# Up projection of a decoder layer: one run of high and low x, and high- and low-weight matmuls by turns

## The reference

```python
    n = rmsnorm(h, mlp_norm_w[l])
    h = h + jnp.square(jax.nn.relu(n @ w_up[l])) @ w_down[l]
return rmsnorm(h, final_norm_w)
```

## Time and profile before

| | |
|---|---|
| median of the timed runs | 1051.15 us |
| profiled execution, span from first to last instruction | 1050.2 us |
| what lies around the span (median less span) | 0.95 us |
| PE busy | 1037.8 us, 99% |
| weight loads (PEld), beside PE | 896.9 us, 85% |
| DVE busy | 637.0 us, 61% |
| ACT busy | 503.3 us, 48% |
| DMA | 190.42 MB, mean 181 GB/s |
| matmuls of L1805 and L1808 | 1024 each |

### The profile page before, as it was taken

The page is one execution under the profiler, slowest core; times in us unless marked ns, Lnnn a source line. Parts: engine busy times, 40 slices in busy tenths (PEclk is TensorE's granted clock), DMA queues, the critical chain, the costliest instruction groups (busy, mean ns, idle before and its releaser), DMA issues.

```text
span 1050.2 us, 14384 instructions
## 1 busy us (share of the span) xinstructions
PE 1037.8 (99%) x5631; PEld 896.9 (85%) x5631; DVE 637.0 (61%) x762; ACT 503.3 (48%) x630; POOL 92.5 (9%) x152
## 2 busy tenths in 40 slices
PE   8999999999999999999999999999999999999996
PEld 7889999888888888888888888888888888888885
DVE  4655986988856554565456456545554555655666
ACT  4655855877754544344334333334433433433434
POOL 2135100633200100000000000000000000000002
PEclk9999999999999999999999999999999999999999
DMA  9576672342346566566556655665566556655662
GB/s 329 181 201 196 210 251 82 133 147 91 111 127 192 164 187 191 186 198 195 186 182 197 197 178 187 197 197 180 184 198 194 182 186 196 197 175 189 199 200 80
DMA packets 89137, 190.42 MB, mean 181 GB/s; under 512 B 8758, under 2 KB 29964, under 8 KB 88716
## 3 DMA queue, kind: packets, MB, share of 16 engines
q1 hardware_dynamic: 88668, 189.41, 56.7%
q10 hardware_dynamic: 432, 0.52, 0.1%
HBM read 187.82 MB, written 2.10 MB: 181 GB/s over the span
## 4 chain that ended last, share of the span: by engine, by line
PE 94%; DVE 3%; ACT 2%; issue 1%; DMA 0%; DVEq 0%; ACTq 0%
PE ps L1805 23%; PE ps L1387 15%; PE ps L1388 15%; PE ps L1391 15%; PE ps L1808 12%; PE ps L1678 2%; PE ps L1679 1%; PE ps L1682 1%; PE ps L1662 1%; PE ps L1460 1%; PE ps L1635 1%; PE ps L1663 1%; PE ps L1513 1%; PE ps L1511 1%; PE ps L1512 1%
## 5 line engine op out<-in xcount | busy, mean ns | idle before, releaser
L885 DVE TENSOR_TENSOR w_lo<-raw,w_hi 128x2048 fp32r<-128x2048 f32 (+4 forms) x198 | 402.3, 2034 | 355.0 <-ACT w_hi L594 289.1
L594 ACT ACTIVATE w_hi<-raw 128x2048 fp32r<-128x2048 f32 x119 | 228.1, 1917 | 399.3 <-PE ps L1391 200.7
L1805 PE MATMUL ps<-xT,w_hi 128*128 128x512 f32 x1024 | 279.3, 394 | 0.0
L1805 PEld LDWEIGHTS ps<-xT,w_hi 128*128 128x128 f32 x1024 | 176.0, 189 | 24.3
L1808 PEld LDWEIGHTS ps<-xT,w_lo 128*128 128x128 f32 x1024 | 157.1, 189 | 21.7
L1387 PE MATMUL ps<-w_hi,hidT 128*128 128x512 f32 x448 | 174.5, 390 | 0.0
L1388 PE MATMUL ps<-w_lo,hidT 128*128 128x512 f32 x448 | 174.4, 389 | 0.0
L1808 PE MATMUL ps<-xT,w_lo 128*128 128x256 f32 x1024 | 162.8, 281 | 0.0
L1391 PE MATMUL ps<-w_hi,hidT 128*128 128x512 f32 x448 | 138.1, 389 | 0.0
L587 ACT ACTIVATE w_hi<-raw 128x1024 fp32r<-128x1024 f32 (+3 forms) x75 | 104.1, 1391 | 68.0 <-PE ps L1391 40.9
L1391 PEld LDWEIGHTS ps<-w_hi,hidT 128*128 128x128 f32 x448 | 84.1, 188 | 17.6
(11 more groups left out here) (339 smaller groups left out, 1268.8 us busy)
## 6 DMA issues: line engine op xcount, KB each, us to landing
raw<-in_w_up SPq DMA_DIRECT2D x64, 1024.0 KB, 5.2
raw<-in_w_down SPq DMA_DIRECT2D x64, 1024.0 KB, 5.4
raw<-in_w_o SPq DMA_DIRECT2D x16, 1024.0 KB, 5.5
raw<-in_w_in SPq DMA_DIRECT2D x8, 1024.0 KB, 5.3
raw<-in_w_in SPq DMA_DIRECT2D x8, 816.0 KB, 4.4
raw<-in_w_in SPq DMA_DIRECT2D x6, 832.0 KB, 8.8
raw<-in_mla_w_uq SPq DMA_DIRECT2D x12, 256.0 KB, 4.6
raw<-in_mla_w_ukv SPq DMA_DIRECT2D x4, 512.0 KB, 4.8
```

Of the source, the lines that this page charges most:

```text
L594: act.activation(w_hi[:, j % SPLIT, :], raw[:, j % RAW, :], ACT.Copy).then_inc(hi_done, 1)
L885: return dve.tensor_tensor(dst, src, high.bitcast(F32), ALU.subtract)
L1805: pe.matmul(both, w_hi[:, slot, 512 * b + P * f:512 * b + P * f + P], xT[:, :, k0 + b, :], start=start and b == 0, stop=False)
```

## The change

`xT` is declared with the part inside the block, so that the low part of a block lies directly behind its high part; all writers and readers have their indices turned. In `up_products` the moving operand of L1805 is then one run of 512 elements and not two of 256, and the destination is the whole bank in one run; the two loops over `b` become one, in which the high-weight matmul and the low-weight matmul of a block follow each other.

```diff
-        xT, Y_AT = seq(X_AT, ("xT", [P, 2, KT, T], F32R))
+        xT, Y_AT = seq(X_AT, ("xT", [P, KT, 2, T], F32R))
...
-                act.activation(xT[:, 0, k, :], bank(4 + k % 4, T), ACT.Copy, scale=wcols[:, k:k + 1]).then_inc(xt_hi, 1)
+                act.activation(xT[:, k, 0, :], bank(4 + k % 4, T), ACT.Copy, scale=wcols[:, k:k + 1]).then_inc(xt_hi, 1)
...
-                return xT[:, part, k, P * t:P * t + P]
+                return xT[:, k, part, P * t:P * t + P]
...
-                        pe.matmul(o, w_hi[:, s, w], xT[:, 0, k, :], start=k == 0 and f == 0, stop=False)
-                        m = pe.matmul(o, w_hi[:, s, w], xT[:, 1, k, :], start=False, stop=False)
+                        pe.matmul(o, w_hi[:, s, w], xT[:, k, 0, :], start=k == 0 and f == 0, stop=False)
+                        m = pe.matmul(o, w_hi[:, s, w], xT[:, k, 1, :], start=False, stop=False)
...
                 for f in range(4):
                     if free is not None:
                         free(f)
-                    both = ps[:, b0 + f, :].rearrange("p (c t) -> p c t", c=2)
                     for b in range(4):
-                        pe.matmul(both, w_hi[:, slot, 512 * b + P * f:512 * b + P * f + P], xT[:, :, k0 + b, :],
+                        w = slice(512 * b + P * f, 512 * b + P * f + P)
+                        pe.matmul(ps[:, b0 + f, :], w_hi[:, slot, w], xT[:, k0 + b, :, :].rearrange("p c t -> p (c t)"),
                                   start=start and b == 0, stop=False)
-                    for b in range(4):
-                        m = pe.matmul(ps[:, b0 + f, 0:T], w_lo[:, slot, 512 * b + P * f:512 * b + P * f + P], xT[:, 0, k0 + b, :],
+                        m = pe.matmul(ps[:, b0 + f, 0:T], w_lo[:, slot, w], xT[:, k0 + b, 0, :],
                                       start=False, stop=stop and b == 3)
                 m.then_inc(w_used, 1)
```

More of the change, by code:

```diff
@@ L774, in turned_hi @@
                 act.wait_ge(ht_t, k + 1)
-                act.activation(xT[:, 0, k, :], bank(4 + k % 4, T), ACT.Copy,
+                act.activation(xT[:, k, 0, :], bank(4 + k % 4, T), ACT.Copy,
                                scale=wcols[:, PRM["mlp"] + k:PRM["mlp"] + k + 1]).then_inc(ht_hi, 1)
@@ L908, in x_lo @@
                 dve.wait_ge(xt_hi, k + 1)
-                low(xT[:, 1, k, :], bank(4 + k % 4, T), xT[:, 0, k, :], wcols[:, k:k + 1]).then_inc(xt_lo, 1)
+                low(xT[:, k, 1, :], bank(4 + k % 4, T), xT[:, k, 0, :], wcols[:, k:k + 1]).then_inc(xt_lo, 1)
             def c_lo(k):
@@ L1207, in turned_lo @@
                 dve.wait_ge(ht_hi, k + 1)
-                low(xT[:, 1, k, :], bank(4 + k % 4, T), xT[:, 0, k, :], wcols[:, PRM["mlp"] + k:PRM["mlp"] + k + 1]).then_inc(ht_lo, 1)
+                low(xT[:, k, 1, :], bank(4 + k % 4, T), xT[:, k, 0, :], wcols[:, PRM["mlp"] + k:PRM["mlp"] + k + 1]).then_inc(ht_lo, 1)
             for c in range(WO_N + 4, MLP0):
@@ L1677, in q_products @@
                         w = slice(256 * b + P * f, 256 * b + P * f + P)
-                        pe.matmul(o, w_hi[:, s, w], xT[:, 0, k, :], start=k == 0 and f == 0, stop=False)
-                        m = pe.matmul(o, w_hi[:, s, w], xT[:, 1, k, :], start=False, stop=False)
+                        pe.matmul(o, w_hi[:, s, w], xT[:, k, 0, :], start=k == 0 and f == 0, stop=False)
+                        m = pe.matmul(o, w_hi[:, s, w], xT[:, k, 1, :], start=False, stop=False)
                         if c == WO_M - 1 and quarter == 3 and k == KT - 1:
                             m.then_inc(first_done, 1)
-                        m = pe.matmul(o, w_lo[:, s, w], xT[:, 0, k, :], start=False, stop=k == KT - 1 and f == 1)
+                        m = pe.matmul(o, w_lo[:, s, w], xT[:, k, 0, :], start=False, stop=k == KT - 1 and f == 1)
                     if quarter == 1 and c in FREED:
```

## The result

The changed kernel takes 1053.06 us (median of 18 runs, 1052.34 to 1054.38) against 1051.29 for the kernel before (18 runs, 1050.93 to 1052.62): ratio 1.0017, 95% interval 1.0010 to 1.0023. It is slower by 1.8 us; the forecast was 2.8 us, 1053.9 us in all, with a range of 1052.3 to 1055.5. The profiled execution has a span of 1050.9 us against 1050.2.

The account below looks back on a forecast made before the run. PE, busy 99% of the 1050.2 us span, was taken as the bound. Order +2.8, layout 0 and elsewhere 0 gave 1053.0; 0.95 around the span made 1053.9 us, own range 1052.3 to 1055.5, wider range 1046.6 to 1056.0.

Parts of the forecast that it names:

- PE bounds, so only start to start counts: Whole kernel: PE busy 99% of the span, never waiting in the loop, so only intervals between matmul starts set the price.
- Its signs: Loop timeline: sixteen pairs in 5.65 us, first 512 behind a down projection still 227 ns; a shorter loop refutes the prediction.
- Layout at zero: Up projection's moving operand as one run instead of two 16 KB apart: no gain, bounded above by 6 us.
- The second rival: Up projection: cost hangs on shares of widths, not order; 350.7 ns a pair stays, 1051.2 us; chance 0.22.
- Its estimate that a load of 107 ns is hidden: Up projection: a 128-column weight load takes 107 ns, as long as a 256 streams, so hidden in either order.
- a worse alternation: Up projection: each 512 at 237 ns, each 256 at 120, 355 ns a pair or more; +6.4 us, 1057.6; chance 0.08.
- Order: toll of 6.7 ns a pair: Up projection: alternation costs 6.7 ns over unmixed prices, as in the input projection; 353.4 against 350.7 ns a pair, +2.8 us.
- On 1024 pairs: Up projection: the extra 2.7 ns was applied to all 1024 pairs of high- and low-weight matmuls, giving +2.8 us.
- No wait changes: Whole kernel: no wait, transfer or semaphore changes and the weight slot's release stays on the last low-weight matmul; 0 us.
- The first rival: Up projection: single 256s between 512s never build up the excess; 346.7 ns a pair, 4.1 us faster, 1047.0; chance 0.28.
- "The finer the two are mixed, the dearer": Rule from the input projection's 512s and 320s: strict alternation costs 6.7 ns a pair, a coarser order 3 ns.

Follow-up runs that it names:

- PE alone: Small kernel without the layer, TensorE only: sections of matmul orders, mostly behind 24 matmuls of 512 columns; alternation took 352.8 ns a pair, or 346.6 behind one transpose.
- sixteen and sixteen: Changed kernel's layout, but each chunk runs all sixteen 512-column matmuls, then all sixteen 256-column ones; 1048.85 us, ratio 0.9977 to the kernel before.
- the snake: Like sixteen and sixteen, but odd chunks begin with their 256-column matmuls, so chunks meet in equal width; 1047.96 us, ratio 0.9967 to the kernel before.
- two and two: Changed kernel's layout, each output tile ordered as two 512s, two 256s, two 512s, two 256s; 1048.90 us, ratio 0.9976 to the kernel before.
- four and four: Order of the kernel before: four 512-column matmuls, then four 256-column ones, per output tile; 350.7 ns a pair, 1051.29 us.
- one transpose: Changed kernel plus one 128-column transpose ahead of each of the loop's 14 up projections; 1051.33 us, ratio 0.9999 to the kernel before.

## Why the prediction was right, and where its size was off

- *PE bounds, so only start to start counts.* Right: PE isn't idle in the loop in any kernel here, and each time followed from the sum of its intervals. Its signs came as written: sixteen pairs in 5.65 us (22.60/4), the first 512 behind a down projection at 0.23 us, and the loop longer and not shorter.
- *Layout at zero.* Right, and shown twice: 1.0000 with the layout alone, equal totals on PE alone.
- *The second rival (order doesn't matter, 350.7 ns a pair either way)* fell: the order alone took the loop to 353.3 and the kernel to 1.0015 (1.0006 to 1.0024). Its estimate that a load of 107 ns is hidden beside any 256 doesn't fit the runs: a load's record lasts 0.19 us, and the price of a pair depends on how wide the loads are (353.1 with 128 columns, 340.0 with 64). The fourth, *a worse alternation* from 355 ns up, wasn't reached.
- *Order: toll of 6.7 ns a pair, taken from the 512/320 alternation.* 353.4 forecast, 353.3 measured in all thirteen up projections behind the first down projection. Borrowing the toll across widths came out by luck as much as by reason: 288 beside 512 has half of it and 224 half as much again, while 320 and 384 have the same.
- *On 1024 pairs.* This factor was mis-sized: it holds for 13 x 64 + 16 = 848. Of the 192 pairs ahead of the first down projection only the first chunk's 16 pay it, since the others entered from transposes (eight each time, and eight gave the cheap cycle on PE alone too). So 848 pairs pay 2.6 ns more than before and 176 pay 4 ns less: 2.2-0.7 = +1.5 us, where 2.8 was forecast and 1.8 was measured. So the slowdown stayed at 0.17%, under the 0.2% that the prediction held for somewhat likelier to be passed (0.39 against 0.34).
- *No wait changes.* Right for this change. Where I moved work myself, in sixteen and sixteen and in the snake, it was wrong to forget the readers of the banks: 0.4 us.
- *The first rival (a run of 256s stores the excess, alternation removes it)* was wrong as a reason, for alternation behind 512s is dear from its second 512 on (on PE alone 227 ns, then 233, then 241), with never more than one 256 in between; its price was real, though, in the stretch ahead of the loop. That one and the same order has two prices stood in no case of mine.
- *"The finer the two are mixed, the dearer"* is the sentence that fell: two and two costs 348.2, four and four 350.7, alternation 353.3 or 346.7.

Open: what in TensorE holds the state. That it is the phase between the loads and the streams at entry is a guess; the runs show only that the same instructions settle in one of two cycles, that with narrow high weights alternation stands at 340.0 even behind 512s, the entry that else leads to the dear one, and that both cycles arise without the other engines. Whether these, or the jump back at the end of the loop body, sway the choice behind one transpose wasn't tested.

## What to carry to other kernels

Where TensorE is never idle, price a reordering by start-to-start differences of the very sequence, widths and predecessor included; a small run of TensorE alone gave the price of each order in the full kernel to 0.2 ns (353.1, 350.9, 348.3 and 347.9 in the settled halves). Runs of equal width, turned so that chunks meet in the same width, were worth 0.3 to 0.4% here (3.4 and 4.3 us by the timed runs, 3.3 and 3.8 by the traces), while strict alternation lost 0.17%. Before putting all long matmuls of a chunk first, look at who still reads their banks.

## What the hardware showed that I had not expected

- Two stable cycles for one instruction stream: H and L by turns at 353.3 ns a pair (237, 117 on average) or 346.7 (232, 115), chosen at entry; 1, 2 and 8 transposes gave the cheap one on PE alone, 3, 4 and none the dear one, and in the full kernel one transpose gave each.
- A settled 512-column matmul costs 226.7 ns with 128 columns of weights, at 2.4 GHz 13.3 more than its columns; a 256 costs 120 with 128 columns of weights and 113 with 64, but a 512 with 64 costs 230.5, more and not less.
- Two runs of 256 elements 16 KB apart stream as fast as one of 512.
